# The order of turn and scores on TensorE in the attention part of a hybrid decoder layer

## The chip, the cores and the metric

The kernel runs on one core of one Trainium2 chip. The metric is the device time of one execution in microseconds (us), lower is better. PE is TensorE, PEld its weight loads, DVE VectorE, ACT ScalarE, POOL GpSimd, SP SyncE, which starts most DMAs.

## What is computed

One decoder layer on 1024 tokens of width 1024, in float32. The change lies in the attention, of which the reference says, cut to what matters:

```python
proj = einsum('bsd,de->bse', rms_norm(x, g), w_in)      # pool, three conv parts, q, k, v
# sliding window of 128, blocks of 128 queries against their own and the previous block of keys
scores = einsum('bnqhgd,bnkhd->bnhgqk', qb, kk) * (HEAD_DIM ** -0.5)
scores = where(mask, scores, NEG_INF)
probs = softmax(concatenate([scores, sink], axis=-1), axis=-1)[..., :2 * BLOCK]
out = einsum('bnhgqk,bnkhd->bnqhgd', probs, vv)         # 8 query heads, 2 kv heads, 64 wide
...
x = x + rms_norm(concatenate([pool, conv, attn]) @ w_o) # then a gated conv MLP
```

## The kernel before, in words

The matmuls with weights split each operand into a high and a low float32r part and use three products (L1513 high by high, L1514, L1515 the cross terms). The program goes through stages one after the other: normalised x, turned and split; the input projection in 14 column tiles; attention; output projection; up projection of the MLP; down projection. All engines run lists of instructions in program order, written out by hand, and meet at semaphores.

Attention runs in the shadow of the input projection. It has 16 units (UNITS): one block b of 128 queries with one kv head, that is four query heads. The list UNIT gives their order. PE runs a loop over 18 slots u (SLOTS). Slot u holds one half of a projection tile n = 5 + u // 2 (two parts of 12 matmuls of 512 columns), and around it the attention work. In the kernel before a slot is, in order:

- score(u), L1621 and L1622: Q by K for unit u into the PSUM banks 4 and 5, eight matmuls. It waits for s_masked, that is, until DVE has read the scores of the unit before.
- turn_probs(u - 1), L1630: four transposes of the normalised probabilities of the unit before into bank 6. It waits for p_norm (L1168 on DVE) and p_masked. In slot 1 this turn stands in the middle of the projection half, and it still does after the change.
- set_free and w_split in even slots, then the first part of the projection half, L1513 to L1515
- in slots 8 and 10 a product of the pool group, L1659; then the second part of the half
- attend(u - 1), L1644 and L1648: probabilities by V into bank 7, with outputs of 64 partitions. It waits for p_masked (L1176, L1178 on DVE).

DVE goes unit by unit in one order: mask_scores(u) (L1152 waits for the copy of the scores by ACT, L765; then L1156, L1157, L1159, the row maximum), mask_probs(u - 1) (L1176, L1178, on the turned probabilities), and norm_probs(u) (L1164, L1166, L1168), which waits for the exponentials of ACT (L773, L776). Between them stand other pieces (mixer_work, low_ring, low_q): low parts of a weight (L1054), Q's low part (L1120) in slot 2, sums of the pool group (L1183, L1207), products of the conv group (L1221, L1229) and its taps (L1237) in slot 11. For units 1, 3 and 9 to 15 norm_probs stands behind these pieces. ACT does the copy of the attended values (L782), the copy of the scores (L765), a weight's high part (L697) and the exponentials.

Of the kernel before, what the change touches and what calls it, by code (L numbers as in the profile page):

```python
# [56 lines left out]
UNITS = len(UNIT)  # L57
# [23 lines left out]
def build(nc, consts, x, norm_mix_pre, w_in, pool_w, pool_scale, conv_w, attn_sinks, w_o,  # L81
# [18 lines left out]
    with ctx:  # L100
# [1408 lines left out]
        def _(pe):  # L1509
# [35 lines left out]
            def project(m, n, c, ks=range(KD)):  # L1545
                return channels(use_banks(m) + c, n % SPLIT, hhi, hlo, half_of(c), ks)
# [33 lines left out]
            def set_free(m):  # L1580

                pe.wait_ge(*taken[m - 2])
# [17 lines left out]
            def score(u):  # L1600

                b, kv = UNIT[u]
                if u >= 1:
                    pe.wait_ge(s_masked, u)
                if u - 1 in POOL_SLOT:
                    pe.wait_ge(pool_out, POOL_SLOT.index(u - 1) + 1)
                if u == 0:
                    pe.wait_ge(k_ready, 2)  # L1610
                    pe.wait_ge(q_ready, 2)
                if u == 3:
                    pe.wait_ge(q_ready, 4)
                first = max(b - 1, 0)
                keys = slice(first * P, (b + 1) * P)
                for e in range(2):
                    for g in range(2):
                        at = g * 2 * P + (first - b + 1) * P
                        acc = ps[:, 4 + e, at:(g + 1) * 2 * P]
                        q = q_parts[:, b, 4 * kv + 2 * g + e, :]  # L1620
                        pe.matmul(acc, q, k_hi[:, kv, keys], start=True, stop=False)  # L1621
                        last = pe.matmul(acc, q, k_lo[:, kv, keys], start=False, stop=True)  # L1622
                last.then_inc(scored, 1)

            def turn_probs(u):
                pe.wait_ge(p_norm, u + 1)
                if u >= 1:
                    pe.wait_ge(p_masked, u)
                for i in range(4):
                    last = pe.transpose(ps[:, 6, i * P:(i + 1) * P], prob[:, u % 2, i, :], ident)  # L1630
                last.then_inc(p_turned, 1)

            def attend(u):
                b, kv = UNIT[u]
                pe.wait_ge(p_masked, u + 1)
                if u == 0:
                    pe.wait_ge(vt_ready, 1)
                if u >= 1:
                    pe.wait_ge(pv_out, u)
                cols = slice(kv * HD, (kv + 1) * HD)  # L1640
                for e in range(2):
                    acc = ps[e * HD:(e + 1) * HD, 7, 0:2 * P]
                    heads = slice(2 * e, 2 * e + 2)
                    last = pe.matmul(acc, v_tok[:, b, cols],  # L1644
                                     pt_cur[:, heads, :].rearrange("p h q -> p (h q)"),
                                     start=True, stop=b == 0)
                    if b:
                        last = pe.matmul(acc, v_tok[:, b - 1, cols],  # L1648
                                         pt_prev[:, heads, :].rearrange("p h q -> p (h q)"),
                                         start=False, stop=True)  # L1650
                last.then_inc(pv_done, 1)

            def pool_product(i):
                if i == 0:
                    pe.wait_ge(pool_w_in, 64)
                pe.wait_ge(pool_ready, i + 1)
                pe.wait_ge(s_masked, POOL_SLOT[i] + 1)
                for c in range(2):
                    last = pe.matmul(ps[:, 4 + c, :], pool_mat[:, i, :],  # L1659
                                     pool_d[:, i, c * HALF:(c + 1) * HALF],  # L1660
                                     start=True, stop=True)
                last.then_inc(pool_mixed, 1)


            for u in range(SLOTS):
                n, c = SLOT0 + u // 2, u % 2
                if u < UNITS:
                    score(u)
                if 2 <= u <= UNITS:
                    turn_probs(u - 1)  # L1670
                if c == 0:
                    set_free(use_of[n])
                    pe.wait_ge(w_split, n + 1)
                project(use_of[n], n, c, range(0, 4))
                if u == 1:
                    turn_probs(0)
                if u in POOL_SLOT:
                    pool_product(POOL_SLOT.index(u))
                last = project(use_of[n], n, c, range(4, KD))
                if c == 1 or n == NIN - 1:  # L1680
                    last.then_inc(proj_done, 1)
                if 1 <= u < UNITS:
                    attend(u - 1)
# [160 lines left out]
```

## Time and profile before

| | us |
|---|---|
| median of 3 runs | 972.93 |
| lowest and highest run | 972.05, 975.95 |
| time of the profiled execution | 972.82 |
| its span | 971.0 |
| busy: PE, PE weight loads, DVE, ACT, POOL | 951.6, 783.6, 651.4, 424.9, 197.9 |
| attention stretch, first scores to last attend | 78.5 to 221.2 |

The span is the time between the first and the last instruction that the profile has. Busy time is a sum over instructions, idle time is given ahead of an instruction with what ended it. The end of a matmul is modelled, so the distances between starts are the safer numbers on PE; a matmul of 512 columns is given 0.39 us, while one starts every 0.23. "issue" is idle time in which an engine waited for nothing that the profile shows.

### The profile page before, as it was taken

How to read it: one execution, taken by the hardware profiler on the slowest of the kernel's cores; microseconds unless marked ns; L12 is line 12 of the kernel's file. 1: busy time of each engine (PE TensorE's matmuls, PEld its weight loads, DVE VectorE, ACT ScalarE, POOL GpSimd, SP SyncE). 2: the span in 40 equal slices, each digit the busy share in tenths (PEclk: the TensorE clock that was granted, in tenths of full speed). 3: DMA queues.
4: the chain of work that ended last, by engine and by line, in shares of the span. 5: the costliest groups of instructions: out<-in, count | busy, mean ns of one | idle time of the engine just before them, and what ended most of it. 6: DMA issues, size and time to landing. Idle time of an engine off the chain costs nothing.

```text
span 971.0 us, 11470 instructions
## 1 busy us (share of the span) xinstructions
PE 951.6 (98%) x4448; PEld 783.6 (81%) x4448; DVE 651.4 (67%) x688; ACT 424.9 (44%) x634; POOL 197.9 (20%) x184
## 2 busy tenths in 40 slices
PE   7999999999999999899999999999999999999997
PEld 6988777776888888688888888888888888888885
DVE  5545786665555399887778778777876653535767
ACT  5524444444333224544444445444444454335352
POOL 2401000000111470522332253434341100000022
PEclk9999999999999999899999999999999999999999
DMA  6799971007322266344343345555455775766557
GB/s 228 241 324 220 214 146 44 23 22 226 108 99 89 87 144 171 114 125 152 98 140 117 132 104 135 129 121 131 108 124 163 214 232 185 257 213 232 166 167 280
DMA packets 114087, 151.14 MB, mean 156 GB/s; under 512 B 6265, under 2 KB 65905, under 8 KB 114033
## 3 DMA queue, kind: packets, MB, share of 16 engines
q1 hardware_dynamic: 100577, 118.63, 37.7%
q0 software_dynamic: 13456, 31.79, 16.4%
q8 instruction: 35, 0.57, 0.2%
q14 instruction: 19, 0.16, 0.1%
HBM read 113.17 MB, written 60.29 MB: 179 GB/s over the span
## 4 chain that ended last, share of the span: by engine, by line
PE 90%; DVE 5%; DMA 3%; ACT 1%; issue 0%; SPq 0%; POOL 0%; DVEq 0%; POOLq 0%; ACTq 0%
PE ps L1513 28%; PE ps L1514 28%; PE ps L1515 28%; DMA r_dram<-cst 1%; PE ps L1523 1%; PE ps L1621 1%; DMA xin<-in_x 1%; PE ps L1644 1%; PE ps L1622 1%; PE ps L1630 1%; DVE r_lo L1382 1%; DMA wraw<-in_w_o 1%; PE ps L1648 1%; DVE yv L1357 0%; DVE hlo L1054 0%
## 5 line engine op out<-in xcount | busy, mean ns | idle before, releaser
L1513 PE MATMUL ps<-hhi,whi 128*128 128x512 f32 (+1 forms) x256 | 95.7, 374 | 2.2 <-DVE hlo L1072 2.2
L1515 PE MATMUL ps<-hhi,wlo 128*128 128x512 f32 (+1 forms) x256 | 93.0, 363 | 0.0
L1514 PE MATMUL ps<-hlo,whi 128*128 128x512 f32 (+1 forms) x256 | 93.0, 363 | 0.0
L595 POOL TENSOR_SCALAR meansq<-sumsq 128x1 f32<-128x1 f32 x28 | 8.8, 314 | 382.2 <-ACT yg L990 170.8
L638 POOL TENSOR_TENSOR w_sums<-wraw 128x1024 f32<-128x1024 f32 x19 | 46.3, 2436 | 187.0 <-DVE h2lo L1397 88.2
L1513 PE MATMUL ps<-h2hi,whi 128*128 128x512 f32 x168 | 65.5, 390 | 0.0
L1514 PE MATMUL ps<-h2lo,whi 128*128 128x512 f32 x168 | 65.4, 389 | 0.0
L1515 PE MATMUL ps<-h2hi,wlo 128*128 128x512 f32 x168 | 65.4, 389 | 0.0
L1513 PEld LDWEIGHTS ps<-hhi,whi 128*128 128x128 f32 x256 | 48.4, 189 | 9.9 <-DVE hlo L1072 2.6
L1515 PEld LDWEIGHTS ps<-hhi,wlo 128*128 128x128 f32 x256 | 48.3, 189 | 7.6
L1514 PEld LDWEIGHTS ps<-hlo,whi 128*128 128x128 f32 x256 | 48.4, 189 | 7.4 <-issue 0.5
L1513 PE MATMUL ps<-hhi,mhi 128*128 128x512 f32 x128 | 51.4, 401 | 2.4 <-DVE hlo L1054 2.4
L1514 PE MATMUL ps<-hlo,mhi 128*128 128x512 f32 x128 | 50.4, 393 | 0.0
L1515 PE MATMUL ps<-hhi,mlo 128*128 128x512 f32 x128 | 50.4, 393 | 0.0
L949 ACT ACTIVATE yg<-ps,par_b 128x1024 f32<-128x1024 f32 x19 | 22.9, 1207 | 55.4 <-DVE ps L1407 55.4
L1513 PE MATMUL ps<-r_hi,h2hi 128*128 128x512 f32 x104 | 41.5, 399 | 4.0 <-DVE h2lo L1397 4.0
L1324 DVE SCALAR_TENSOR_TENSOR yg<-ps,par_a,yg 128x1023 f32<-128x1023 f32 x22 | 28.2, 1282 | 25.4 <-ACT yg L949 25.4
L1338 DVE TENSOR_TENSOR wlo<-wraw,whi 128x1024 fp32r<-128x1024 f32 x23 | 27.8, 1223 | 25.1 <-ACT whi L979 24.8
L1514 PE MATMUL ps<-r_lo,h2hi 128*128 128x512 f32 x104 | 41.4, 398 | 0.0
L1515 PE MATMUL ps<-r_hi,h2lo 128*128 128x512 f32 x104 | 41.3, 397 | 0.0
L1513 PE MATMUL ps<-r_hi,w2hi 128*128 128x512 f32 x104 | 40.5, 390 | 0.0
L1515 PE MATMUL ps<-r_hi,w2lo 128*128 128x512 f32 x104 | 40.5, 389 | 0.0
(229 smaller groups left out, 2650.1 us busy)
## 6 DMA issues: line engine op xcount, KB each, us to landing
wraw<-in_ffn_w_up SPq DMA_DIRECT2D x44, 512.0 KB, 5.2
s_dram<-in_ffn_w_down POOLq DMA_DIRECT2D x6, 2816.0 KB, 28.2
wraw<-r_dram SPq DMA_DIRECT2D x44, 256.0 KB, 3.4
wraw<-s_dram SPq DMA_DIRECT2D x44, 256.0 KB, 4.2
r_dram<-cst SPq DMA_DIRECT2D x33, 256.0 KB, 2.8
wraw<-act_dram SPq DMA_DIRECT2D x33, 256.0 KB, 3.6
wraw<-in_ffn_w_down SPq DMA_DIRECT2D x33, 256.0 KB, 4.3
wraw<-in_w_in SPq DMA_DIRECT2D x14, 512.0 KB, 11.0
```

The costliest lines, as they stand in the source:

```text
L638: pool.tensor_tensor(w_sums[:, 0:2, :], raw[:, 0:4:3, :], raw[:, 2:3, :].broadcast_to([P, 2, HALF]), ALU.add)\
L949: act.activation(yg[:, pair % 2, :], banks(4 * (pair % 2)), ACT.Identity, bias=ffn_bias(pair), scale=ffn_tap(2, pair)).then_inc(yg_started, 1)
L1324: finish_step(dve.scalar_tensor_tensor(y[:, 1:], src[:, :SEQ - 1], ffn_tap(1, f), y[:, 1:], ALU.mult, ALU.add))
L1338: dve.tensor_tensor(lo, raw, hi, ALU.subtract).then_inc(d_split, 1)
L1382: dve.tensor_tensor(r_lo[i][:, :, :, :].rearrange("p t k c -> p t (k c)"), made(i), r_hi[i][:, :, :, :].rearrange("p t k c -> p t (k c)"), ...
L1513: pe.matmul(acc, w_hi, x_hi, start=first, stop=False, skip_group_check=looped)
L1514: pe.matmul(acc, w_hi, x_lo, start=False, stop=False, skip_group_check=looped)
L1515: return pe.matmul(acc, w_lo, x_hi, start=False, stop=last, skip_group_check=looped)
L1523: last = pe.transpose(ps[:, b + k // 4, (k % 4) * P:(k % 4 + 1) * P], rows[:, k * P:(k + 1) * P], ident)
L1621: pe.matmul(acc, q, k_hi[:, kv, keys], start=True, stop=False)
L1622: last = pe.matmul(acc, q, k_lo[:, kv, keys], start=False, stop=True)
L1630: last = pe.transpose(ps[:, 6, i * P:(i + 1) * P], prob[:, u % 2, i, :], ident)
```

## The change

In the loop over the slots turn_probs(u - 1) now stands ahead of score(u).

```diff
@@ -1664,10 +1664,10 @@
 
             for u in range(SLOTS):
                 n, c = SLOT0 + u // 2, u % 2
+                if 2 <= u <= UNITS:
+                    turn_probs(u - 1)
                 if u < UNITS:
                     score(u)
-                if 2 <= u <= UNITS:
-                    turn_probs(u - 1)
                 if c == 0:
                     set_free(use_of[n])
                     pe.wait_ge(w_split, n + 1)
```

Only PE's list changes, and only in slots 2 to 15. In slot 3 it is this (+ is the changed kernel; L1644 and L1648 are attend(1), L1621 and L1622 score(3), L1630 turn_probs(2)):

```order
 L1644 MATMUL ps<-pt_cur,v_tok 64x256
 L1648 MATMUL ps<-pt_prev,v_tok 64x256
+L1630 MATMUL ps<-cst,prob 128x128 x4
 L1621 MATMUL ps<-k_hi,q_parts 128x128
 L1622 MATMUL ps<-k_lo,q_parts 128x128
...
 L1621 MATMUL ps<-k_hi,q_parts 128x128
 L1622 MATMUL ps<-k_lo,q_parts 128x128
-L1630 MATMUL ps<-cst,prob 128x128 x4
 L1513 MATMUL ps<-hhi,whi 128x512
 L1514 MATMUL ps<-hlo,whi 128x512
```

The four transposes have moved from behind the eight score matmuls to ahead of them. In slot 12 the list of before, with the semaphores that an instruction waits for, is this, from the end of attend(10) to the projection:

```order
L1644 MATMUL ps<-pt_cur,v_tok 64x256
L1648 MATMUL ps<-pt_prev,v_tok 64x256
L1621 MATMUL ps<-k_hi,q_parts 128x256 [waits scores_masked]
L1622 MATMUL ps<-k_lo,q_parts 128x256
...
L1622 MATMUL ps<-k_lo,q_parts 128x256
L1630 MATMUL ps<-cst,prob 128x128 [waits probs_masked,probs_normed]
L1630 MATMUL ps<-cst,prob 128x128 x3
L1513 MATMUL ps<-hhi,whi 128x512 [waits w_split,conv_in_ready]
```

and of the changed kernel this:

```order
L1644 MATMUL ps<-pt_cur,v_tok 64x256
L1648 MATMUL ps<-pt_prev,v_tok 64x256
L1630 MATMUL ps<-cst,prob 128x128 [waits probs_masked,probs_normed]
L1630 MATMUL ps<-cst,prob 128x128 x3
L1621 MATMUL ps<-k_hi,q_parts 128x256 [waits scores_masked]
L1622 MATMUL ps<-k_lo,q_parts 128x256
...
L1622 MATMUL ps<-k_lo,q_parts 128x256
L1513 MATMUL ps<-hhi,whi 128x512 [waits w_split,conv_in_ready]
```

The wait for probs_normed now stands ahead of the wait for scores_masked and of all matmuls behind it.

## Rows read from the trace of the kernel before

**Rows 1.** The page's first part: busy time, share of span, instructions by engine.

```profile
PE 951.6 (98%) x4448; PEld 783.6 (81%) x4448; DVE 651.4 (67%) x688; ACT 424.9 (44%) x634; POOL 197.9 (20%) x184
```

**Rows 2.** By window: length, busy PE, PEld, DVE, ACT, POOL (count), PEclk, DMA, GB/s.

```profile
92.47:208.55 116.08, 116.08 (x622) 89.72 (x621) 83.91 (x155) 53.50 (x170) 1.47 (x1) 1.00 0.50 103
...
233.70:236.40 2.70, 2.70 (x6) 2.15 (x7) 1.15 (x2) 0.00 (x0) 0.00 (x0) 0.50 1.13 295
```

**Rows 3.** Timeline, PE, slot 15: start, us, engine, line, operation, [idle before].

```profile
200.47 0.39 PE L1621 MATMUL ps<-k_hi,q_parts 128*128 128x256 f32 x1
...
201.53 0.60 PE L1630 MATMUL ps<-cst,prob 128*128 128x128 f32 x4
...
202.20 0.39 PE L1514 MATMUL ps<-hlo,whi 128*128 128x512 f32 x1
```

**Rows 4.** Timeline, PE, slot 16.

```profile
208.55 0.66 PE L1630 MATMUL ps<-cst,prob 128*128 128x128 f32 x4
...
209.28 0.40 PE L1514 MATMUL ps<-hlo,whi 128*128 128x512 f32 x1
```

**Rows 5.** Timeline, PE, slot 1.

```profile
84.90 0.28 PE L1621 MATMUL ps<-k_hi,q_parts 128*128 128x256 f32 x1
...
86.08 0.40 PE L1514 MATMUL ps<-hlo,whi 128*128 128x512 f32 x1
```

**Rows 6.** Timeline, DVE L1168 of units 2, 4, 11, 12; PE, slots' first scores.

```profile
100.35 0.69 DVE L1168 TENSOR_TENSOR prob<-prob,small 128x512 f32<-128x512 f32 x1
...
100.57 0.33 PE L1621 MATMUL ps<-k_hi,q_parts 128*128 128x128 f32 x1
...
114.52 0.69 DVE L1168 TENSOR_TENSOR prob<-prob,small 128x512 f32<-128x512 f32 x1
...
116.19 0.39 PE L1621 MATMUL ps<-k_hi,q_parts 128*128 128x256 f32 x1
...
176.07 0.69 DVE L1168 TENSOR_TENSOR prob<-prob,small 128x512 f32<-128x512 f32 x1
...
176.23 0.39 PE L1621 MATMUL ps<-k_hi,q_parts 128*128 128x256 f32 x1
...
183.77 0.69 DVE L1168 TENSOR_TENSOR prob<-prob,small 128x512 f32<-128x512 f32 x1
...
184.31 0.39 PE L1621 MATMUL ps<-k_hi,q_parts 128*128 128x256 f32 x1
```

**Rows 7.** Timeline, DVE, slots 2, 11 and 12.

```profile
94.36 0.74 DVE L1152 COPY_PREDICATED s_sb<-cst,ps 128x512 f32<-128x512 uint32 x1 [2.70 <-ACT s_sb L765]
...
170.04 0.75 DVE L1152 COPY_PREDICATED s_sb<-cst,ps 128x512 f32<-128x512 uint32 x1 [3.47 <-ACT s_sb L765]
...
173.03 2.60 DVE L1237 SCALAR_TENSOR_TENSOR gate_y<-conv_in,par_a,gate_y 128x1023 f32<-128x1023 f32 x2
...
178.12 0.75 DVE L1152 COPY_PREDICATED s_sb<-cst,ps 128x512 f32<-128x512 uint32 x1 [1.36 <-ACT s_sb L765]
```

**Rows 8.** Timeline, DVE and PE, the hand-over at two later waits of PE.

```profile
232.42 1.23 DVE L1054 TENSOR_TENSOR hlo<-wraw,hhi 128x1024 fp32r<-128x1024 f32 x1 [2.84 <-ACT hhi L697]
...
233.70 0.79 PE L1513 MATMUL ps<-hhi,mhi 128*128 128x512 f32 x1 [2.40 <-DVE hlo L1054]
...
325.06 1.28 DVE L1316 SCALAR_TENSOR_TENSOR hrow_c<-x2b,rstd,gain_b 128x1024 f32<-128x1024 f32 x1 [0.99 <-POOL rstd L598]
...
326.50 1.07 PE L1523 MATMUL ps<-cst,hrow_c 128*128 128x128 f32 x8 [0.51 <-DVE hrow_c L1316]
```

**Rows 9.** The waits of PEld, 76 to 222 us: us in total, times, longest.

```profile
PEld ps L1644 <- issue: 5.6, 16, 0.4
...
PEld ps L1621 <- issue: 5.4, 14, 0.4
```

**Rows 10.** The chain that ended last, behind the last attend.

```profile
221.22 0.39 ACT mix_att L782
...
224.97 6.34 DMA wraw<-in_w_o
```

## The prediction

> **What bounds the kernel now.** I read the page first: TensorE (PE) is busy 98% of the 971.0 us span, VectorE (DVE) 67% [rows 1]. Then the busy time by window, for the stretch from the scores of unit 2 to the last turn, 92.47 to 208.55 us: PE is busy in all 116.08 us, at a granted clock of 1.00 (2.4 GHz) [rows 2]. The table of waits has no PE row for another engine between 78 and 221 us, only its own short "issue" gaps [rows 9]. So here the end is set by PE's own list of instructions. An edit to its order can win only what PE loses when it goes from one kind of work to another, and it can lose as soon as PE has to wait for a result.
>
> I call the pass of the loop with index u slot u, and its start the moment at which attend(u-2), the last work of the slot before, has been issued. In the old order slot u starts with the scores of unit u (L1621), and the turn of unit u-1 (L1630) stands behind them. A full slot takes 8.08 us (176.23 to 184.31 [rows 6]). Slots 2 to 15, fourteen of them, change their order. Slots 0 and 1 do not, nor does slot 16, which has a turn and no scores.
>
> **Part 1: the same instructions in another order.** Nothing is added or removed, no DMA is moved, and each instruction keeps its waits. What each piece costs in issue time:
> - Old slot 15: first score at 200.47, first transpose at 201.53, so 1.06 for the scores; the second projection matmul is at 202.20, so turn plus one matmul take 0.67 [rows 3]. A projection matmul in a steady row takes 0.23, which leaves 0.44 for the turn. Together 1.50.
> - A turn straight behind attend stands in the old trace too, in slot 16: 208.55 to 209.28 with one projection matmul, 0.73, so 0.50 for the turn [rows 4].
> - Scores with ordinary matmuls on both sides stand in slot 1: 84.90 to 86.08, again with one projection matmul, 1.18, so 0.95 for the scores [rows 5].
>
> The new order is the last two in a row: 0.50 + 0.95 = 1.45, a gain of 0.05 a slot. Its bounds: if the scores pay the same start-up behind transposes as they pay behind attend (1.06), a slot loses 0.06; if neither pays any (0.44 + 0.95), it gains 0.11. I take 0.05, because each of its two parts is a row. Over 14 slots this is -0.70 us, between +0.84 and -1.54.
>
> The one costly thing at these borders is the idle gap of the weight loads: 5.6 us ahead of 16 attends, 5.4 ahead of 14 scores, 0.35 and 0.39 each [rows 9]. In the old slot 16 the turn behind attend has the same gap, which is why I let the gap pass from scores to turn and count no gain. The Trainium skill, TensorEngine Tiling (Array Packing), section Key Properties, says that changing the tiling mode drains TensorE; attend writes 64 columns, turn, scores and projection all 128. By that rule two drains a slot stay two, as in the sum; a reader who took the gap for a switch between number formats would expect a third gap between turn and scores, which is the second rival.
>
> **Part 2: the wait that the turn now has.** The turn of unit u-1 waits for its normalised probabilities (L1168 on DVE). In the old order the scores gave it 1.06 us more. Now it comes at the slot's start, and everything behind it on PE, the scores and then the projection and attend, queues behind that wait. I compared the end of L1168 with the start of the slot that needs it, for all units:
> - unit 2: ends 100.35 + 0.69 = 101.04, slot 3 starts at 100.57: late by 0.47 [rows 6];
> - unit 11: ends 176.07 + 0.69 = 176.76, slot 12 starts at 176.23: late by 0.53 [rows 6];
> - unit 12: ends 183.77 + 0.69 = 184.46, slot 13 starts at 184.31: late by 0.15 [rows 6];
> - unit 4: ends 115.21, slot 5 starts at 116.19: early by 0.98 [rows 6]. Units 6 and 14 have the same 0.98, units 1 and 9 have 0.82 and 1.07, all others 1.35 or more.
>
> On top of this the probabilities come later than before. The scores are now finished 1.45 after the slot's start and no longer 1.06, so 0.39 later, and DVE is bound to them: it sat idle until the copied scores came in slots 2, 11 and 12 (2.70, 3.47 and 1.36 us), and works without a pause from there to L1168 in all three. What makes these slots late is one extra piece: two subtractions of Q of 2.46 us in slot 2, the convolution taps of 2.60 in slot 11 [rows 7], a weight's low part and the gated product in slot 12. The earlier turn gives DVE nothing in return: in its order the mask on the turned probabilities (L1176) stands behind the mask on the next scores (L1152), which come later. This is why the move cannot speed up DVE.
>
> From the end on DVE to the start on PE I count 0.10: 233.65 to 233.70 is 0.05, 326.34 to 326.50 is 0.16 [rows 8]. The slot would have begun 0.05 sooner (part 1). So the waits are
> - slot 3: 101.04 + 0.39 + 0.10 - 100.52 = 1.01;
> - slot 12: 176.76 + 0.39 + 0.10 - 176.18 = 1.07;
> - slot 13: 184.46 + 0.39 + 0.10 - 184.26 = 0.69 (both ends are counted from the scores of slot 12, so the wait there does not help).
>
> Sum 2.77 us, between 2.6 and 3.0 with 0.05 to 0.16 for the hand-over. In slot 5 and its like 0.98 - 0.39 - 0.10 - 0.05 leaves 0.44 in hand, and slot 2, whose probabilities come from an unchanged slot 1, has 0.82 - 0.10 = 0.72: no wait. The Trainium skill, TensorE: Matmul & The Clock Gate, step 1 of Part 2, says that weight loads may be pulled ahead but matmuls stay in program order. By that rule the scores cannot pass the waiting turn, and at most a load of some 0.19 us hides in the wait; the trace of before has no such wait on a turn to show it.
>
> **What follows behind.** Attend needs the masked probabilities only at the end of its slot: by the timeline the mask ends 1.7 us or more ahead of it in every slot, so 0.39 later is covered by the projection between them; without that cover it would be 0.39 a slot. The output projection behind the attention waits on a chain that starts at the last attend: its copy at 221.22, then pieces of w_o, with a load of 6.34 us [rows 10]. That chain is tied to PE's progress, so a delay passes through to the end and is not swallowed.
>
> **Sum:** 2.77 - 0.70 = +2.1 us. On the profiled execution's own time, 972.82 us (span 971.0), this gives 974.9; the median of the runs is 0.1 higher, so I say 975.0. The bounds of both parts give 973.9 to 976.7.
>
> **Rivals.**
> 1. *No wait appears, only the 0.05 a slot.* 972.9 - 0.7 = 972.2. It needs DVE's chain in slots 2, 11 and 12 not to hang on the scores, or the scores to pass the turn. The idle time of DVE ahead of L1152 speaks against it. 6%.
> 2. *Slower beyond 0.5%: a start-up between turn and scores.* If the fp32 transposes and the scores behind them needed the gap that they have behind attend, 0.39 in each of 14 slots, that is 5.4 more: 980.4. It decides from 0.2 us a slot (4.9 - 2.1 = 2.8 over 14). Against it: from turn to projection, the same switch of formats, the trace has no gap in any slot. 3%.
> 3. *The waits let the clock fall.* Behind the wait of 2.40 us at 233.70 the granted clock was 0.50 (1.2 GHz) for 2.70 us [rows 2, 8], about 1.35 lost. One wait of 1 us with this effect gives 976.4, all three 979.1, which is slower beyond 0.5%. Against it: the wait of 0.51 at 326.50 left the clock full, and mine are of 1 us. 8% for one or two, 2% for all.
> 4. *The wait spreads.* If hand-over and shift are together 0.45 larger than I count, slots 5, 7 and 15 wait as well, and the three late ones wait 0.45 longer: about +1.4 to +2, so 976.9. The 0.39 is bounded by rows on both sides. 8%.
> 5. *Somewhere else 2 to 5 us are won*, for instance by w_o loads that fall better after the shift, 0.5% faster or more. Nothing in the trace shows such a reserve in PE. 2%.
>
> My forecast keeps 71%. Within 0.5% (4.9 us, about what a measurement of this kernel can tell from no change) lie the forecast, rival 1, rival 4 and most of rival 3. So: faster 2%, slower 5% (rival 2 and the end of rival 3), no difference 93%. The range takes in the bounds of the sum, one fall of the clock and the spread rival, and below it half of the way to rival 1: 973.0 to 977.4.
>
> **What the changed profile should show.** PE in the attention stretch: three rows of waiting ahead of L1630 with DVE's L1168 as releaser, near 101.5, 177 and 185, of 0.7 to 1.1 us; none in the other slots. From the first transpose to the first score 0.50, from there to the projection 0.95. A full slot without wait of 8.03. DVE's idle time ahead of L1152 longer by 0.4 a slot. The rest of the profile the same, later by 2 us. I would be wrong in the mechanism if slots 3 and 12 had no wait, and wrong in part 1 if a slot without a wait took over 8.2 or under 7.9.

## The result and the profile after

Over 22 runs of each kernel the changed one takes 973.83 us in the median (972.12 to 977.17) and the one before 971.62 (970.19 to 975.95). The ratio is 1.0023 with a 95% interval of 1.0014 to 1.0032: 2.2 us slower, between 1.4 and 3.1. That is clear of zero with so many runs and well inside the 0.5% within which I had put it. The profiled execution has a span of 974.2 us where [rows 1] belong to one of 971.0. Its first lines, span and busy time by engine:

```profile
span 974.2 us, 11470 instructions
...
PE 952.2 (98%) x4448; PEld 783.7 (80%) x4448; DVE 651.5 (67%) x688; ACT 425.5 (44%) x634; POOL 198.6 (20%) x184
```

TensorE works as long as before (952.2 and 951.6 us). What it did not do before is wait inside the attention stretch. This is the table of waits from 76 to 226 us, of PE and its weight loads (total us, times, longest). The same table of the kernel before has no row for PE, and for the weight loads the gaps of [rows 9]:

```profile
PE ps L1630 <- DVE prob L1168: 2.4, 3, 1.0
...
PEld ps L1644 <- issue: 5.6, 16, 0.4
...
PEld ps L1630 <- issue: 4.6, 12, 0.4
...
PEld ps L1630 <- DVE prob L1168: 3.8, 3, 1.4
```

Three turns wait for L1168, 2.4 us in all. The "issue" gap of 0.38 us that stood ahead of 14 scores now stands ahead of the turns, and no gap is left ahead of the scores. The Trainium skill, TensorEngine Tiling (Array Packing), section Key Properties, speaks of a drain at a change of tiling mode: by that rule attend keeps two drains a slot, and the trace agrees with two gaps: 0.35 us ahead of each attend (5.6 over 16) and 0.38 behind it (4.6 over 12). That the gap is a drain no run here shows.

One of the three waits, slot 3 in the timeline (start, us, engine, line). The rows are attend, L1168, the turn's weight loads, the turn and the first score:

```profile
99.82 0.66 PE L1644 MATMUL ps<-pt_cur,v_tok 128*64 128x256 f32 x4
...
101.08 0.69 DVE L1168 TENSOR_TENSOR prob<-prob,small 128x512 f32<-128x512 f32 x1
...
101.82 0.42 PEld L1630 LDWEIGHTS ps<-cst,prob 128*128 128x128 f32 x4 [1.37 <-DVE prob L1168]
...
101.83 0.66 PE L1630 MATMUL ps<-cst,prob 128*128 128x128 f32 x4 [0.91 <-DVE prob L1168]
...
102.24 0.31 PE L1621 MATMUL ps<-k_hi,q_parts 128*128 128x128 f32 x1
```

Attend starts at 99.82, so an unhindered turn would start 1.02 later, at 100.84. That is the distance in every slot without a wait, but for slots 2 and 5: their attend has half the matmuls, and there it is 0.58. L1168 ends at 101.77 and the turn starts at 101.83: 0.99 us lost. I count a wait in this way from start to start; the 0.91 in brackets is shorter because the end of the attend matmul is modelled. Slot 12 lost 1.03 and slot 13 0.64 by the same count, 2.66 together. Their attends and turns:

```profile
175.97 0.66 PE L1644 MATMUL ps<-pt_cur,v_tok 128*64 128x256 f32 x4
...
178.02 0.66 PE L1630 MATMUL ps<-cst,prob 128*128 128x128 f32 x4 [0.96 <-DVE prob L1168]
...
185.03 0.66 PE L1644 MATMUL ps<-pt_cur,v_tok 128*64 128x256 f32 x4
...
186.69 0.66 PE L1630 MATMUL ps<-cst,prob 128*128 128x128 f32 x4 [0.57 <-DVE prob L1168]
```

A slot without a wait, slot 15, which answers to [rows 3]:

```profile
202.74 0.65 PE L1630 MATMUL ps<-cst,prob 128*128 128x128 f32 x4
...
203.15 0.36 PE L1621 MATMUL ps<-k_hi,q_parts 128*128 128x256 f32 x1
203.36 0.28 PE L1622 MATMUL ps<-k_lo,q_parts 128*128 128x256 f32 x1
...
204.18 0.39 PE L1513 MATMUL ps<-hhi,whi 128*128 128x512 f32 x1
...
204.41 0.40 PE L1514 MATMUL ps<-hlo,whi 128*128 128x512 f32 x1
```

Turn 0.41, scores 1.03 up to the first projection matmul, 1.67 up to the second where it was 1.73. The attend of slot 15 is 8.02 behind that of slot 14 where it was 8.08. So the new order gives back 0.06 a slot.

The busy time by window (length, then busy PE, PEld, DVE, ACT, POOL with counts, clock, DMA share, GB/s): first scores to last attend, from there to the end of the wait for w_o, and the rest. First the changed kernel, then the one before:

```profile
78.84:222.28 143.44, 140.99 (x745) 109.60 (x744) 101.91 (x182) 65.67 (x199) 4.54 (x3) 1.00 0.48 99
...
222.28:236.07 13.79, 11.11 (x51) 8.17 (x50) 7.95 (x9) 7.45 (x9) 0.00 (x0) 0.99 0.85 263
...
236.07:974.20 738.13, 725.92 (x3214) 600.25 (x3214) 503.05 (x464) 319.62 (x386) 178.74 (x147) 0.99 0.52 152
```

```profile
78.50:220.07 141.57, 141.57 (x746) 110.31 (x744) 101.96 (x182) 65.45 (x199) 4.54 (x3) 1.00 0.49 101
...
220.07:233.70 13.63, 11.21 (x51) 8.18 (x50) 7.95 (x9) 7.45 (x9) 0.00 (x0) 0.99 0.85 260
...
233.70:971.00 737.30, 725.88 (x3214) 600.29 (x3214) 502.98 (x464) 319.33 (x386) 178.10 (x147) 0.99 0.52 152
```

The first stretch is 1.87 us longer, and PE's busy time in it is 0.6 shorter. The rest is 0.2 and 0.8 longer. That rest cannot be put down to the change: over the nine profiled executions of this study the time from the last attend to the end lies anywhere from 748.8 to 753.2 us, with the same code behind the attention (the shortest at a mean granted clock of 0.997 over the execution, the longest at 0.991). The attention stretch, on the other hand, comes out within 0.1 us of what issue times and waits add up to (2.66 - 14 x 0.06 = 1.82 here), and within 0.4 in the furthest of the runs below. This is why the experiments below are read by that stretch first and by their ratio second.

### The profile page after: what moved, and what is told of

Its sections match the earlier page's. It is cut to its first block, busy times and chain, and to the rows that moved or that the text cites. A ratio compares the mean times of both kernels' runs of the same rounds, so it can differ in the third digit from the quotient of the medians.

```text
span 974.2 us, 11470 instructions
## 1 busy us (share of the span) xinstructions
PE 952.2 (98%) x4448; PEld 783.7 (80%) x4448; DVE 651.5 (67%) x688; ACT 425.5 (44%) x634; POOL 198.6 (20%) x184
## 4 chain that ended last, share of the span: by engine, by line
PE 85%; DVE 7%; DMA 3%; ACT 1%; POOL 1%; issue 1%; SPq 0%; DVEq 0%; POOLq 0%; ACTq 0%
PE ps L1513 27%; PE ps L1515 27%; PE ps L1514 27%; DMA r_dram<-cst 1%; PE ps L1523 1%; DMA xin<-in_x 1%; PE ps L1630 1%; PE ps L1644 1%; PE ps L1622 1%; PE ps L1621 1%; DVE r_lo L1382 1%; DMA wraw<-in_w_o 1%; DVE w2lo L1397 1%; PE ps L1648 0%; DVE yv L1357 0%
```

## Experiments

Each edit is shown against the changed kernel; only the last run starts from the kernel before. The stretch named below runs from the first scores to the start of the last attend: 141.57 us before, 143.44 after, each time read from one profiled execution.

**The theory** (A in the expectations): three units' probabilities end late on DVE; the turn that comes earlier waits for them, a bit longer because the scores are 0.39 later; the order itself gives 0.06 a slot back. **The rivals:** the new order has a cost in every slot that the issue times do not show, or the loss lies behind the attention (B); and, within A, that the late scores play no part, or that ACT and not the order on DVE makes the probabilities late.

### Old order in the three slots

```diff
             for u in range(SLOTS):
...
-                if 2 <= u <= UNITS:
+                late = u in (3, 12, 13)
+                if 2 <= u <= UNITS and not late:
                     turn_probs(u - 1)
                 if u < UNITS:
                     score(u)
+                if late:
+                    turn_probs(u - 1)
```

> The turn goes ahead of the scores in 11 slots; slots 3, 12 and 13, the three with a wait, keep the old order. Theory A (three waits of 0.99, 1.03 and 0.64 us cost the time, the new order itself gives back about 0.06 a slot): no wait of PE for L1168, full slots of 8.02, last attend at 0.06 x 11 = 0.7 us before that of the kernel before; ratio to before 0.9993. Theory B (the new order costs something in every slot that the issue times do not show, or the loss comes from behind the attention): still slower than before by 1 to 2 us, ratio 1.001 to 1.002.

Ratio 0.9990 (0.9977 to 1.0003); stretch 141.04 us. The waits of PE from 76 to 240 us:

```profile
PE ps L1513 <- DVE hlo L1054: 2.7, 1, 2.7
```

That is the wait for w_o behind the attention and the only row: none for L1168. Eleven slots in the new order cost nothing, and the stretch is 0.53 us shorter than before, of 0.7 expected. So PE's new order, left out in the three late slots, is by the stretch a small gain with nothing changed on DVE; the interval of the ratio still includes no difference. Rival B wanted a ratio above 1.001, and the interval ends below that: it falls.

### New order only in the three slots

The reverse: the turn goes ahead in slots 3, 12 and 13 alone.

```diff
-                if 2 <= u <= UNITS:
+                late = u in (3, 12, 13)
+                if late:
                     turn_probs(u - 1)
                 if u < UNITS:
                     score(u)
+                if 2 <= u <= UNITS and not late:
+                    turn_probs(u - 1)
```

> The turn goes ahead of the scores only in slots 3, 12 and 13. Theory A, with the late scores as a part of the wait: units 2 and 11 are scored in unchanged slots, so slot 3 waits 101.04 + 0.06 - 100.57 = 0.53 and slot 12 176.76 + 0.06 - 176.23 = 0.59; unit 12 is scored 0.39 later in slot 12, so slot 13 waits 0.6 to 0.65. Sum 1.75, less 3 x 0.06: +1.6 us, ratio 1.0016. If the waits come from the earlier turn alone and the later scores play no part, the waits stay at 0.99, 1.03 and 0.64: +2.5. Theory B: +0.4 or less.

Ratio 1.0017 (1.0003 to 1.0031); stretch 143.17, which is +1.60 us. The waits, and the turn of slot 12:

```profile
PE ps L1630 <- DVE prob L1168: 1.5, 3, 0.6
...
178.18 0.66 PE L1630 MATMUL ps<-cst,prob 128*128 128x128 f32 x4 [0.51 <-DVE prob L1168]
```

From start to start the three waits are 0.53, 0.59 and 0.65 (slot 12: attend at 176.57, turn at 178.18, 1.61 less 1.02). In the changed kernel slots 3 and 12 wait 0.99 and 1.03. The difference of 0.46 and 0.44 is what the later scores of the slot before add (0.39), with the 0.06 by which those slots are shorter. So the three waits are the whole loss, and in two of them four tenths come from the scores and not from the turn. (Slot 13 follows a slot in the new order in both kernels, so its 0.64 and 0.65 do not separate the two.)

### The scores still later

```diff
-                if u < UNITS:
+                if u < 2:
                     score(u)
...
-                project(use_of[n], n, c, range(0, 4))
+                project(use_of[n], n, c, range(0, 1))
+                if 2 <= u < UNITS:
+                    score(u)
+                project(use_of[n], n, c, range(1, 4))
```

> The changed kernel, but from slot 2 on the scores stand behind the turn and the first three projection matmuls, so 0.68 us later. Theory A: the three waits grow by 0.68 each, and slots 5, 7, 10 and 15, which have 0.47 to 0.51 in hand in the changed kernel, wait about 0.2 each: 2.8 us more than the changed kernel, 4.7 to 5.0 more than before, ratio 1.005. If the wait in a slot does not hang on when the slot before issued its scores: no more than the changed kernel, ratio 1.002.

Ratio 1.0044 (1.0029 to 1.0059); stretch 146.55, +4.98. The waits, then attend and turn of slot 7:

```profile
PE ps L1630 <- DVE prob L1168: 4.5, 3, 1.6
...
134.44 0.66 PE L1644 MATMUL ps<-pt_cur,v_tok 128*64 128x256 f32 x4
...
135.66 0.66 PE L1630 MATMUL ps<-cst,prob 128*128 128x128 f32 x4
```

The large waits are now 1.66, 1.70 and 1.33 from start to start, each 0.67 to 0.69 longer than in the changed kernel. The small ones are too short for the table, but the starts show them: 134.44 to 135.66 is 1.22 where 1.02 is free, so 0.20 in slot 7; 0.20, 0.14 and 0.20 in slots 5, 10 and 15. Sum 5.43, which is 2.77 more than in the changed kernel, of 2.8 expected. The stretch is 0.39 longer than this sum less 14 x 0.06: a full slot without a wait takes 8.05 here and not 8.02, which accounts for it. The margin that I had computed for those slots is real, and 0.7 us is enough to use it up.

### The mask first on DVE

```diff
             for u in range(UNITS):
+                if u >= 2:
+                    mask_probs(u - 1)
                 mask_scores(u)
                 if u == 0:
                     low_q(2)
-                if u >= 1:
+                if u == 1:
                     mask_probs(u - 1)
```

> The changed order on PE, and on DVE from unit 2 on the mask on the turned probabilities (L1176, L1178) goes ahead of the mask on the next scores (L1152), into the idle time in which DVE waits for the copied scores. Theory A, with DVE's order as the reason that the late slots are late: the 1.3 us of that mask leave the path from the scores to L1168 in slots 2, 11 and 12, all three waits go, all full slots 8.02; 0.06 x 14 = 0.8 us less than before, ratio 0.9992. If the probabilities are late for another reason (ACT's exponentials): waits of 0.5 us or more stay in two or three slots and the ratio is 1.001 or more.

Ratio 1.0009 (0.9995 to 1.0022); stretch 142.30, +0.73. Half a hit. The waits (this file has two lines more, so the turn is L1632), DVE in slot 2, and DVE in slot 6:

```profile
PE ps L1632 <- DVE prob L1168: 1.0, 2, 0.7
...
93.82 0.69 DVE L1176 TENSOR_TENSOR pt_cur<-ps,cst 128x512 f32<-128x512 f32 x1 [1.52 <-PE ps L1632]
...
95.41 0.73 DVE L1152 COPY_PREDICATED s_sb<-cst,ps 128x512 f32<-128x512 uint32 x1 [0.30 <-ACT s_sb L765]
...
127.53 0.68 DVE L1176 TENSOR_TENSOR pt_cur<-ps,cst 128x512 f32<-128x512 f32 x1
...
128.73 0.74 DVE L1152 COPY_PREDICATED s_sb<-cst,ps 128x512 f32<-128x512 uint32 x1
...
132.80 0.69 DVE L1168 TENSOR_TENSOR prob<-prob,small 128x512 f32<-128x512 f32 x1
```

In slot 2 the mask on the turned probabilities runs at 93.82, in DVE's idle time, and L1152 still has to wait for the scores (0.30). The waits of slots 3, 12 and 13 are gone: the order on DVE did make those units late. But I had expected no other wait, and slots 7 and 8 lost 0.77 and 0.36 instead, and the pool product of slot 8, which needs the masked scores, about 0.3. In slot 6 DVE comes from the sums of the pool group at 127.53 with the scores already copied (L765 ends at 127.01), and the mask pushes L1152 back to 128.73, 1.20 later, and L1168 to 132.80. Where DVE has no idle time the mask ahead is not free.

### The mask first in three units only

The same, for units 2, 11 and 12 alone.

```diff
             for u in range(UNITS):
+                ahead = u in (2, 11, 12)
+                if ahead:
+                    mask_probs(u - 1)
                 mask_scores(u)
                 if u == 0:
                     low_q(2)
-                if u >= 1:
+                if u >= 1 and not ahead:
                     mask_probs(u - 1)
```

> The changed order on PE, and on DVE the mask on the turned probabilities ahead of the mask on the next scores only for units 2, 11 and 12, whose L1168 ends late. In the run with that order in all units the waits of slots 3, 12 and 13 went and slots 7 and 8 got waits of 0.7 and 0.3. Theory: DVE was idle ahead of L1152 in units 2, 11 and 12, so the mask is free there, and it was busy until the scores had come in units 5 to 8, so the mask there pushed everything back. Expected: no wait of PE for L1168 anywhere, full slots of 8.02, first scores to last attend 0.8 us shorter than before (140.7 to 140.8), 2.7 shorter than changed; ratio to before 0.9992. If the waits of slots 7 and 8 have another cause they stay, and the stretch is about as long as before.

Ratio 0.9988 (0.9977 to 0.9999), median 970.72 us beside 971.47; stretch 140.81, 0.76 less than before and 2.63 less than the changed kernel. The waits, DVE in slot 11 and the turn of slot 12:

```profile
PE ps L1516 <- DVE hlo L1054: 1.6, 1, 1.6
...
168.90 0.69 DVE L1176 TENSOR_TENSOR pt_cur<-ps,cst 128x512 f32<-128x512 f32 x1 [1.84 <-PE ps L1633]
...
170.49 0.76 DVE L1152 COPY_PREDICATED s_sb<-cst,ps 128x512 f32<-128x512 uint32 x1 [0.29 <-ACT s_sb L765]
...
175.32 0.69 DVE L1168 TENSOR_TENSOR prob<-prob,small 128x512 f32<-128x512 f32 x1
...
176.23 0.66 PE L1633 MATMUL ps<-cst,prob 128*128 128x128 f32 x4
```

No turn waits. L1168 of unit 11 ends at 176.01, and the turn starts at 176.23, on its own time. This version is ahead of both kernels, by the stretch 0.8 us ahead of the one before; the interval of its ratio only just excludes no difference, so the size rests on the profile. What it gains is PE's order, 14 x 0.06 = 0.84; DVE's new order only takes the waits away. The run with the old order in the three slots has 0.53 of it without touching DVE, and the ratios of the two (0.9988 and 0.9990) do not tell them apart.

### Normalising first in two units

```diff
-                if 4 <= u < 9:
+                if 4 <= u < 9 or u in (11, 12):
                     norm_probs(u)
                 mixer_work(u)
-                if u in (0, 1, 3) or u >= 9:
+                if u in (0, 1, 3, 9, 10) or u >= 13:
                     norm_probs(u)
```

> The changed order on PE. On DVE, for units 11 and 12 alone, the three instructions that end in L1168 go ahead of the conv group's piece (the taps L1237, 2.6 us, and the gated product L1229, 1.1 us), as they do for units 4 to 8. Theory A (those pieces make units 11 and 12 late): no wait in slots 12 and 13, the wait of 0.99 in slot 3 stays; first scores to last attend 1.7 us shorter than in the changed kernel and 0.2 longer than in the one before; ratio to before 1.0002. If the late scores or the exponentials bind those units: waits of 0.5 us stay, and the ratio is 1.001 to 1.002.

Ratio 1.0004 (0.9996 to 1.0013); stretch 141.79, +0.22. The waits, then L1164 and L1168 of unit 11:

```profile
PE ps L1630 <- DVE prob L1168: 0.9, 1, 0.9
...
174.84 0.16 DVE L1164 TENSOR_TENSOR small<-small 128x4 f32<-128x4 f32 x1 [0.60 <-ACT small L776]
...
175.25 0.69 DVE L1168 TENSOR_TENSOR prob<-prob,small 128x512 f32<-128x512 f32 x1
```

Only the wait of slot 3 is left (1.0 from start to start). L1168 of unit 11 now ends at 175.94 and not at 177.96. So in slots 12 and 13 it was the convolution's pieces that stood in the way: ACT's exponentials are ready at 174.84, two microseconds ahead of where L1164 stood in the changed kernel (176.86). With the pieces gone DVE waits 0.60 for them, so ACT comes next. This tells the same as the run before by another edit, since 1.65 us came back of the 1.67 lost there. To take either piece of work out of the way, the mask or the convolution's, is enough to have these two units in time.

### The mask first with PE's old order

The change of DVE's order in all units, put on the kernel before. There is one execution of it, the profiled one, and so no ratio.

> PE in the order of before, and on DVE the mask on the turned probabilities ahead of the mask on the next scores from unit 2 on. Here the turn is issued 1.06 us later in a slot, behind the scores, so the mask cannot fill DVE's idle time: it starts about 1.7 after the slot's start and L1152 about 1.1 later than before. PE has 1.06 us more at each turn, so no wait for L1168; a wait of up to 1 us at the pool product in slot 8, which needs the scores masked. First scores to last attend 0 to 1 us longer than before. If DVE's order alone were worth something, it would be shorter.

Stretch 142.81, +1.24, of 0 to 1 expected. The wait of PE, and L1152 of unit 2:

```profile
PE ps L1661 <- DVE s_sb L1152: 1.0, 1, 1.0
...
95.52 0.75 DVE L1152 COPY_PREDICATED s_sb<-cst,ps 128x512 f32<-128x512 uint32 x1
```

No turn waits, and the pool product of slot 8 waits 1.0 us for the masked scores. L1152 starts 2.90 behind the slot's scores (92.62) and not 1.89 as before. DVE's order gives nothing by itself: with the turn behind the scores the mask starts too late to fit into DVE's idle time. PE's new order in all slots costs 1.9 us, DVE's alone, in all units, 1.2, and both together, DVE's in three units only, gain 0.8. (DVE's in three units alone was not run with PE's old order.)

## Why the prediction was right, point by point

- **What bounds the stretch.** PE's own list. Held: each variant follows from issue times and waits of PE, to within 0.4 us of the stretch.
- **The order itself.** Forecast 0.05 a slot within -0.06 to +0.11, measured 0.06. It is split otherwise than I added it: turn 0.41 and scores 1.03, where I had 0.50 and 0.95. In the old slot 16 I had taken 0.23 off for the projection matmul behind the turn, but there that matmul took 0.32:

```profile
208.96 0.48 PE L1513 MATMUL ps<-hhi,whi 128*128 128x512 f32 x1
```

The turn was 0.41 there too (208.55 to 208.96), and 0.09 lay on the first matmul behind it (208.96 to 209.28). In the new order that 0.09 falls on the first score (203.15 to 203.36, 0.21, where the next ones are 0.12 apart), and the projection matmul behind the scores is back at 0.23. I had put the 0.09 on the turn and left it off the scores, so the sum came out right although both parts were off.
- **Which slots wait.** Slots 3, 12 and 13 and no other, as the comparison of L1168's end with the slot's start said.
- **How long.** Forecast 1.01, 1.07 and 0.69, measured 0.99, 1.03 and 0.64. The term that was a little too large is the hand-over from DVE to PE: I took 0.10 between 0.05 and 0.16 [rows 8], and it was 0.06, 0.06 and 0.05. The shift by the later scores was 0.39 as computed (L1168 of unit 2 ends 8.57 us behind its slot's start before, 8.96 after).
- **Sum.** Forecast +2.07, by the attention stretch +1.87, by the ratio +2.2 with 0.9 to either side, which is too wide to tell 1.87 from 2.07. The 975.0 us was forecast on a median of 972.93 from three runs; the median of 22 was 971.62, so 973.83 lies lower than 975.0 by the base and not by the difference.
- **A sign that I gave wrongly.** I said that DVE's idle time ahead of L1152 would grow by 0.4 in every slot. It did not; in slots 2, 3 and 11 of the changed kernel it reads

```profile
95.09 0.73 DVE L1152 COPY_PREDICATED s_sb<-cst,ps 128x512 f32<-128x512 uint32 x1 [3.10 <-ACT s_sb L765]
...
103.99 0.74 DVE L1152 COPY_PREDICATED s_sb<-cst,neg_big 128x512 f32<-128x512 uint32 x1 [1.08 <-ACT s_sb L765]
...
171.24 0.75 DVE L1152 COPY_PREDICATED s_sb<-cst,ps 128x512 f32<-128x512 uint32 x1 [3.42 <-ACT s_sb L765]
```

where it was 2.70, 0.17 and 3.47. In slot 11 the piece ahead ends as much later as the scores do, so nothing grows. It grows where the slot before was in the old order (slot 2) and behind a wait (slots 3, 12, 13). This did not touch the sum, which counted the ends and not the idle time.
- **The rivals.** "No wait" and "a start-up between turn and scores" are excluded by the rows of slots 3 and 15. The clock stayed at 1.00 through the whole stretch, waits of 1 us included. "The wait spreads" did not happen; the run with the scores 0.68 later shows the slots 5, 7 and 15 that it named as next, and slot 10, which it had left out. No run shows a gain of 2 to 5 us elsewhere (rival 5).
- **The load in the wait.** I let a weight load of some 0.19 us hide in the wait. A load of the turn is 0.14 us, and the turn's loads in fact started with it (101.82 and 101.83).
- **What follows behind.** That a delay passes through to the end fits the largest one: with the scores still later the stretch is 4.98 longer and the ratio 1.0044 (1.0029 to 1.0059), which is 2.8 to 5.7 us. A part of under 2 us that is swallowed could not be seen.

## What to carry to other kernels

Before an instruction with a wait is moved ahead on a busy in-order engine, compare for each pass of the loop when its input ends and when the new place comes, with the shift of everything that is moved behind it: here eleven passes had at least 0.8 us in hand and three had none, and these three made up the whole result. To keep the old order in those three was enough to turn a loss of 1.9 us into a gain of 0.5 by the stretch. Then look at the order on the engine that uses the result. DVE took its pieces in the old order, so the earlier turn was worth nothing to it; to change its order too, only where it stood idle, removed the waits and made the gain 0.8. Changed everywhere, it made new waits.

## What the runs showed of the hardware

The border from attend (64 output partitions) to work with 128 has the same gap of 0.38 us in the weight loads, whether scores (5.4 us over 14) or transposes (4.6 over 12) follow. Between transposes and the scores behind them there is no such gap: only the first score takes 0.21 and not 0.12, and the scores together 1.03 and not 0.95. Why the first matmul behind the transposes is 0.09 slower, in both orders, no run shows. The weight load of a waiting turn is not taken ahead of the wait: it starts at 101.82, with the matmul at 101.83. There the load may need the probabilities itself, by their place in the kernel's pe.transpose. But at the wait for w_o [rows 8] the load brings in mhi, which ACT had written by 216.68, and it too started only when the wait ended, with its matmul. In the kernel before, ACT's writing of mhi and that load:

```profile
216.07 0.61 ACT L841 ACTIVATE mhi<-mix_att 128x512 fp32r<-128x512 f32 x1
...
233.70 0.29 PEld L1513 LDWEIGHTS ps<-hhi,mhi 128*128 128x128 f32 x1 [2.84 <-DVE hlo L1054]
```

The Trainium skill, TensorE: Matmul & The Clock Gate, step 1 of Part 2, lets weight loads be pulled ahead of matmuls in flight. It does not speak of a matmul that waits at a semaphore; these rows show no load ahead of a wait, and do not contradict it. Waits of PE of 0.14 to 0.20 us did not show in the table of waits of the run with the scores later, since the ends of matmuls are modelled; the distances between starts show them.
